# Weight pieces stored one contiguous run per partition, in a one-core hybrid encoder step

## The reference

```
a = rmsnorm(h);  z = a @ w_in                       # 1024 x 3600, one projection for all groups
o_a = gated delta rule on 4 heads x 128 (causal conv of width 4, chunks, gated norm)
o_b = forgetting attention on 8 heads x 64
h += concat(o_a, o_b) @ w_out                       # 1024 x 1024
x = rmsnorm(h);  q = x @ peer_wq                    # 1024 x 2048
e, gate = top 16 of 128 x 128 product keys, for each of 8 heads and each token
h += sum over 128 picks of gate * gelu(peer_u[e] . x) * peer_v[e]
h += (p @ w_ple_proj) * sigmoid(rmsnorm(h) @ w_ple_gate)     # 256 x 1024, 1024 x 1024
y = rmsnorm(h)
```

## Time and profile before

| | |
|---|---|
| time, median of 3 runs | 4420.42 us (4418.73 to 4431.06) |
| span of the profiled execution, first to last instruction | 4446.2 us (no other time of it is given) |
| PE busy | 2995.1 us, 67% |
| DVE busy | 3329.5 us, 75% |
| ACT busy | 853.4 us, 19% |
| POOL busy | 2797.1 us, 63% |
| bytes moved | 1454.21 MB, mean 327 GB/s |

### The profile page before, as it was taken

One profiled execution on the slowest core, in us unless ns is written; L12 is line 12 of the kernel. 1 busy time (PEld: TensorE's weight loads), 2 busy tenths in 40 slices (PEclk: granted clock), 3 DMA queues, 4 the chain that ended last, 5 costly groups with the idle time before them and its releaser, 6 DMA issues. The chain is left out here.

```text
span 4446.2 us, 39840 instructions
## 1 busy us (share of the span) xinstructions
PE 2995.1 (67%) x12882; PEld 2055.5 (46%) x12882; DVE 3329.5 (75%) x6429; ACT 853.4 (19%) x1663; POOL 2797.1 (63%) x2350
## 2 busy tenths in 40 slices
PE   6736566765777576786678576877688575756556
PEld 5634343543455354554355354554365344535222
DVE  3477878777977787687877887787868785687764
ACT  2112111221122111221122112221122112211111
POOL 1037766577657865677657855676657764686674
PEclk9868788987988788987888888878898797878777
DMA  5269998999999998999899998989899999999996
GB/s 178 90 232 365 331 373 321 370 318 359 348 343 355 313 380 308 369 323 363 321 361 337 341 380 303 375 309 375 311 379 329 353 347 260 373 326 372 270 378 243
DMA packets 632283, 1454.21 MB, mean 327 GB/s; under 512 B 64528, under 2 KB 344016, under 8 KB 632080
## 3 DMA queue, kind: packets, MB, share of 16 engines
q0 software_dynamic: 313344, 1140.99, 70.2%
q1 hardware_dynamic: 317424, 305.92, 21.0%
q10 hardware_dynamic: 1312, 4.72, 0.3%
HBM read 1441.69 MB, written 9.51 MB: 326 GB/s over the span
## 5 line engine op out<-in xcount | busy, mean ns | idle before, releaser
L484 POOL DMA_INDIRECT ring<-peer_u,idx_c x1061 | 1354.5, 1277 | 681.6 <-issue 339.3
L1425 DVE CUSTOM_DVE_ANT_0 ring<-ring,xn_c 128x1024 f32<-128x1024 f32 x1088 | 1349.6, 1259 | 489.8 <-DMA ring<-peer_u,idx_c 440.6
L484 POOL DMA_INDIRECT ring<-peer_v,idx_c x1088 | 1235.5, 1136 | 676.5 <-PE bank L1032 354.6
L1032 PE MATMUL bank<-ring,diag 128*128 128x512 f32 x1920 | 1125.8, 723 | 616.7 <-DMA ring<-peer_v,idx_c 565.6
L1433 DVE SCALAR_TENSOR_TENSOR h_c<-ring,wgt,h_c 128x1024 f32<-128x1024 f32 x608 | 800.5, 1317 | 179.8 <-DMA ring<-peer_v,idx_c 173.5
L1032 PEld LDWEIGHTS bank<-ring,diag 128*128 128x128 f32 x1920 | 401.7, 226 | 1130.1 <-DMA ring<-peer_v,idx_c 730.3
L796 PE MATMUL bank<-aT,wring 128*128 128x128 f32 x4608 | 617.0, 300 | 156.0 <-DMA wring<-w_in 68.6
L796 PEld LDWEIGHTS bank<-aT,wring 128*128 128x128 f32 x4608 | 605.2, 215 | 213.7 <-DMA wring<-w_in 75.3
L800 PE MATMUL bank<-wring,aT 128*128 128x256 f32 (+1 forms) x1440 | 383.5, 428 | 121.7 <-DMA wring<-w_in 68.6
L800 PEld LDWEIGHTS bank<-wring,aT 128*128 128x128 f32 x1440 | 308.4, 218 | 210.8 <-DMA wring<-w_in 85.2
L752 ACT ACTIVATE diag<-ident,wgt 128x128 f32<-128x128 f32 x480 | 178.8, 393 | 300.2 <-PE bank L1032 223.0
(11 more groups left out here) (264 smaller groups left out, 3042.1 us busy)
## 6 DMA issues: line engine op xcount, KB each, us to landing
wring<-w_in SPq DMA_DIRECT2D x108, 1024.0 KB, 15.1
wring<-peer_wq SPq DMA_DIRECT2D x72, 1024.0 KB, 20.4
wring<-w_out SPq DMA_DIRECT2D x36, 1024.0 KB, 18.0
wring<-w_ple_gate SPq DMA_DIRECT2D x36, 1024.0 KB, 13.7
wring<-w_in SPq DMA_DIRECT2D x18, 1056.0 KB, 7.8
ring<-peer_v,idx_c POOLq DMA_INDIRECT x1088, 6.9
ring<-peer_u,idx_c POOLq DMA_INDIRECT x1061, 7.3
wring<-w_ple_proj SPq DMA_DIRECT2D x18, 512.0 KB, 15.0
```

Source lines behind the costliest of these rows:

```text
L484: pool.indirect_dma_start(out=ring[0:rows, n % RING, :], out_offset=None, in_=t["peer_" + kind], in_offset=bass.IndirectOffsetOnAxis(ap=id ...
L1032: last = pe.matmul(YB[g][0:peer, :], diag[0:peer, m % DIAGS, 0:peer], ring[0:peer, r, 512 * g:512 * g + 512], start=(m == 0), stop=(m == l ...
L1425: v.tensor_tensor_reduce(out=row, in0=row, in1=xn_c[0:peer, :], scale=1.0, scalar=0.0, op0=ALU.mult, op1=ALU.add, accum_out=dots[0:peer, k ...
```

## The change

The host lays out every piece as its own input, `piece_<name>`, of 128 partitions with 8 blocks of 256 columns in a row (2048 floats, 8 KB; the `proj` pieces 1024 floats, the ones of 264 columns 2112). The load of a piece is then a copy of this tensor. The five whole matrices are no longer inputs. What lands in `wring` is the same as before.

```diff
-        mats = {"gate": t["w_ple_gate"], "proj": t["w_ple_proj"], "out": t["w_out"], "wq": t["peer_wq"]}
-
         def load_piece(sp, n, name, loaded):
 
-            what, c, w = PIECES[name]
-            src = mats.get(what, t["w_in"])[0].rearrange("(k p) n -> p k n", p=P)
-            k = src.shape[1]
-            sp.dma_start(wring[:, n % WRING, 0:k * w].rearrange("p (k n) -> p k n", k=k),
-                         src[:, :, c:c + w]).then_inc(loaded, 16)
+            src = t["piece_" + name]
+            sp.dma_start(wring[:, n % WRING, 0:src.shape[1]], src).then_inc(loaded, 16)
...
+PROJECTIONS = ("w_in", "w_out", "peer_wq", "w_ple_proj", "w_ple_gate")
...
-    for name in _INS:
-        a = _np.ascontiguousarray(inputs[name])
+    weights = dict(gate="w_ple_gate", proj="w_ple_proj", out="w_out", wq="peer_wq")
+    tiled = {}
+    for name, (what, c, w) in PIECES.items():
+        a = _np.asarray(inputs[weights.get(what, "w_in")])[0, :, c:c + w]
+        tiled["piece_" + name] = a.reshape(-1, P, w).transpose(1, 0, 2).reshape(P, -1)
+    plain = {name: inputs[name] for name in _INS if name not in PROJECTIONS}
+    for name, a in {**plain, **tiled}.items():
+        a = _np.ascontiguousarray(a)
         arrays[name] = a
```

## The result

The changed kernel ran in 4373.35 us (median, 4366.28 to 4382.23) against 4419.57 us for the kernel before in the same rounds: a ratio of 0.9895 with an interval of 0.9864 to 0.9925. A second job with more rounds gave 0.9893 (0.9874 to 0.9912), some 47 us. The forecast was 119 us faster, 4300. The sign was right, the forecast gain 2.5 times the measured one.

A forecast was written before the change was run, and what follows sets the result against it. It took DMA engines to bound A and C, DVE to bound D; 82 us for fewer packets, 36 for sooner weights and 1 at the start made 119 off 4420, so 4300 us, range 4210 to 4410.

The forecast's parts named there:

- What bounds the kernel: Loop pass, after the first tile: two stretches wait for DMA engines, one for DVE, one has hardly a weight load.
- A: Stretch of input projections and the tail's gates, 160 us a pass: bound by DMA engines, share 0.99.
- D: Stretch of the top-16 picks, 80 us a pass: bound by DVE, busy for 76.6 us.
- B: Stretch of the attention work in a pass: loads almost no weights, so hardly touched.
- Fewer packets, their price: Weight loads: seven of eight packets go, each with 8.0 ns fixed cost; 82 us gained over eight passes.
- A and C are bound by these engines, so they count in full.: Saved packet time in both stretches, 7.9 and 2.4 us a pass, counts wholly as run time: 82 us.
- C: Stretch of output projection and first query pieces, 60 us a pass: bound by DMA engines, share 1.04.
- sooner weights: In A, late weights cause a third of 13 us idle DMA capacity: 4.5 us a pass, 36 us in all.
- The rival of bursts: Where DVE is the bound, as in D, long weight pieces delay gathers 2.2 us each: 94 us slower, 4514; chance 0.11.
- A's two terms: In A: fewer packets, 7.9 us a pass, and weights coming sooner, 4.5 us a pass.
- D at nothing: The 2.7 us a pass of packet time saved in D count as no gain, since DVE covers it.
- What would show it: Signs: 73,200 packets, pieces landing in 6 to 8 us, PE's weight waits under 60, A and C 10 to 20 shorter.

The follow-up runs named there:

- run1k: Kernel before with pieces laid out in contiguous blocks of 128 rows but still read as 8 runs of 1 KB: 0.9998 of the kernel before.
- out_new: Kernel before with only the output projection and query pieces as one 8 KB run, the rest loaded from whole matrices: 1.0031, 14 us slower.
- before again: Second profiled execution of the unchanged kernel before: span 4430.0 us, 1.0001 of the kernel before in its job.
- late_out: Changed kernel with output projection and query pieces loaded one projection later: 4356.15 us, 0.9837 of the kernel before.
- best1: Kernel before with input and tail pieces as 8 KB runs, except a pass's first three, which like output and query pieces keep 1 KB runs: 4352.88 us, 0.9816.
- in_new: Changed kernel with output projection and query pieces loaded from whole matrices as before, input and tail pieces still 8 KB runs: 0.9864 of the kernel before.
- late_in: Changed kernel with input projection and tail pieces loaded one projection later: 1.0139 of the kernel before, 109 us slower than the change.

## Why the prediction was too large, point by point

*What bounds the kernel* held as far as it went: A has a DMA share of 1.03 before, D has DVE at 79.5 of 89 us, B has no part. What it left out is how close DVE stands behind the DMA engines in A.

*Fewer packets, their price.* Right, and low: 144 us of engine time freed where 122 were forecast. 8 KB packets exist and cost what the line from 1 KB and 4 KB said: 326 ns in the mean over the changed kernel's trace, 321 by the line. An estimate by the cycles of the Trainium skill's page "DMA: Bandwidth & Descriptors" ("Why small descriptors are slow (HBM only)") is 7.5% less, half of the 15% of the trace (790 against 934 us). The 512 B for line rate on the same page of the Trainium skill (Specifications) are not borne out for 1 KB runs: run1k, with the same inputs and bytes, is at 0.9998 where the change is at 0.9893.

*"A and C are bound by these engines, so they count in full."* This step failed, in both places. For C I counted 2.4 us a pass, 19 in all; it gave none (55.4 and 55.7 us against 55.3), and out_new, with long runs for the output and query pieces alone, is 14 us slower. For A 82 - 19 + 36 = 99 us had been put on fewer packets and sooner weights, 12.4 a pass; over the eight passes it gave 61 to 68 (1261.6 us before again, 1200.2 and 1193.3 in the change; 8 less if run1k's trace stands for before). Two things stood in the way, and the runs show both. One is DVE, which is busy for 111 of A's 148 us: with its products halved A gives 12.4 a pass. The other is that long pieces bunch. A piece lands in 8.3 us, so PE finishes its projections one after the other, their loads are issued together, and weights take bytes from the gathers when both DVE and PE live from them. With the output pieces held back (late_out) A gives 83 us over the eight passes, and with short runs for them (best1, in_new) 82 to 88. In C the rows come 5 us late and are caught up later.

The rival of bursts had this mechanism, with its place in D and a price of 2.2 us a piece. Its places were the end of A, by late_out, and, with long input pieces, the first three pieces of a pass at the end of D. As run time that is some 0.15 us a piece for out_new (14 us over 96 pieces of eight passes) and 0.8 us for those three (20 us over 24). It takes both the long run and the loads drawn together: with 1 KB runs three pieces ahead leave the picks 92 to 96 at 16.4 us (in_new), with 8 KB runs they take 21.5, with one piece less ahead 18.4.

*A's two terms* can't be told apart: the freed engine time was larger than forecast, and so sooner weights may have added little. late_in shows that late weights can cost a lot, but not that they did before.

*D at nothing* held: 90.5 and 91.5 us against 90.2, with the DMA share down. But the end of D was no neutral place: the three first pieces, which I counted with A's, cost there (picks 120 to 127: 23.3 and 23.5 us against 22.4).

*The sum.* Forecast 119, measured 47. Of the 72 us between, 34 are the losses that best1 mends (0.9816 against 0.9893), and 35 come back when DVE is lightened. These two were not tried together, so they may overlap.

*What would show it:* packets, PE's waits for weights and D came as told, landing nearly (8.3 us where 6 to 8 were told); "A and C together 10 to 20 us shorter" did not (9). A gather's landing did not grow over the whole run (`v`: 6.5 us against the earlier trace rows), but it did in A, by 2 us in the pass of the windows above (`u` 8.5 to 10.2, `v` 8.6 to 10.8).

## What to carry to other kernels

A cheaper transfer frees engine time; whether the run gets it back is decided stage by stage, by what stands next behind the DMA engines. Where two queues share the DMA engines and the kernel lives from one of them, making the other faster also makes it greedier: count how many of its loads will now be issued together, and hold them back (one less ahead was worth 25 us here, for the pieces that were bunched; for the input pieces it cost 109) or leave them slow where the first queue can't spare the bytes. The length of an engine's waits does not give their price: 125 us of waits for weights went with 109 us of run time in late_in, and taking 190 away with 47 in the change. Read the DMA share of the stage beside the waits.

## What the runs showed of the hardware

A longer run gave a queue a larger share of the bytes beside another queue: with 8 KB runs weights had 2.74 of 7.37 MB in a stretch where they had 1.54 of 6.86 with 1 KB runs, in part because one more piece was issued in it, and a piece landed after 8.3 us in the median in place of 16. That 8 KB runs and 4 KB rows take turns one for one is not shown. A packet of 8 KB took 326 ns in the mean (change), eight of 1 KB 392 (before again). Contiguous blocks of 128 KB gave nothing over rows of 1 KB strided through a matrix (run1k). SyncE's instruction for a piece was hardly cheaper with an eighth of the runs (0.33 against 0.37 us).
